# DeltaNet's triangular inverse: the 16x16 diagonal blocks are inverted on VectorE over 32 partitions, reached through DRAM, and TensorE does the levels 16, 32 and 64

## What is computed

```
qkv = silu(causal_depthwise_conv(proj[..., :DN_CONV_DIM], conv_w))
...
decay = exp(where(tri, g[..., :, None] - g[..., None, :], -inf))
k_beta = k * beta[..., None]
lower = where(strict, einsum("bhncd,bhnkd->bhnck", k_beta, k) * decay, 0.0)
a_mat = lower + eye(CHUNK)
sol = triangular_solve(a_mat, rhs, left_side=True, lower=True, unit_diagonal=True)
...
def step(state, xs):            # scan over the chunks
    v_new = u_n - w_n @ state
    o = q_n @ state + a_n @ v_new
    state = state * exp(gl_n) + k_n.T @ v_new
```

## Time and profile before

| | us |
|---|---|
| median of the 3 runs (lowest to highest) | 1511.27 (1500.47 to 1516.33) |
| the profiled execution's own time | 1499.67 |
| its span (first to last instruction) | 1497.7 |
| outside the span | 1.97 |
| DeltaNet's steps, of the span | about 51 to 454 |

### The profile page before, as it was taken

How to read it: one execution, slowest core, us unless ns; L and a number is a source line. 1 busy time by engine, 2 the same in 40 slices (tenths; PEclk the granted TensorE clock), 3 DMA queues, 4 the chain that set the end, 5 groups by cost and what they waited for, 6 DMA issues and landing times.

```text
span 1497.7 us, 19380 instructions
## 1 busy us (share of the span) xinstructions
PE 1455.9 (97%) x7270; PEld 1202.1 (80%) x7270; DVE 801.1 (53%) x1132; ACT 541.9 (36%) x820; POOL 268.0 (18%) x269
## 2 busy tenths in 40 slices
PE   7899999999989999999999999999999999999998
PEld 5788888888877888888888777866888888888877
DVE  5555666666647434334356587556443443434655
ACT  7334343434225314232243442244341322314344
POOL 5644444535203100000002120000200000000211
PEclk9999999999999999999999999769999999999998
DMA  6212121110112232323222328511323223232221
GB/s 174 60 29 57 29 57 40 44 49 21 43 56 92 92 112 85 112 84 103 94 85 86 111 57 169 113 29 43 113 85 112 85 92 105 84 112 85 85 85 56
DMA packets 163810, 120.73 MB, mean 81 GB/s; under 512 B 44417, under 2 KB 161442, under 8 KB 163746
## 3 DMA queue, kind: packets, MB, share of 16 engines
q1 hardware_dynamic: 152210, 116.71, 26.1%
q10 hardware_dynamic: 11536, 3.15, 1.0%
HBM read 112.50 MB, written 2.10 MB: 77 GB/s over the span
## 4 chain that ended last, share of the span: by engine, by line
PE 79%; DVE 10%; ACT 4%; issue 3%; DVEq 1%; DMA 1%; ACTq 1%; SPq 1%; POOL 0%; POOLq 0%
PE psum L148 22%; PE psum L150 22%; PE psum L149 21%; PE psum L830 3%; PE psum L821 3%; DVE wL L140 2%; ACT wH L132 1%; PE psum L837 1%; DVE bL L1274 1%; ACT taps L676 1%; DVE hT L1475 1%; PE psum L1828 1%; DVE acc L1473 1%; PE psum L784 1%; PE psum L785 0%
## 5 line engine op out<-in xcount | busy, mean ns | idle before, releaser
L148 PE MATMUL psum<-aH,wH 128*128 128x512 f32 x896 | 363.0, 405 | 5.2 <-DVE wL L140 3.2
L150 PE MATMUL psum<-aL,wH 128*128 128x512 f32 x896 | 350.6, 391 | 0.0
L149 PE MATMUL psum<-aH,wL 128*128 128x512 f32 x896 | 349.9, 391 | 0.0
L140 DVE TENSOR_TENSOR wL<-wRaw,wH 128x2048 fp32r<-128x2048 f32 (+2 forms) x126 | 250.7, 1993 | 135.5 <-ACT wH L132 129.9
L148 PE MATMUL psum<-bH,wH 128*128 128x512 f32 x720 | 285.0, 396 | 5.7 <-DVE pleT L1909 3.2
L150 PE MATMUL psum<-bL,wH 128*128 128x512 f32 x720 | 280.8, 390 | 0.0
L149 PE MATMUL psum<-bH,wL 128*128 128x512 f32 x720 | 280.6, 390 | 0.0
L132 ACT CAST wH<-wRaw 128x2048 fp32r<-128x2048 f32 (+2 forms) x110 | 199.2, 1815 | 192.0 <-PE psum L150 191.8
L148 PEld LDWEIGHTS psum<-aH,wH 128*128 128x128 f32 x896 | 169.2, 189 | 37.1 <-DVE wL L140 3.4
L150 PEld LDWEIGHTS psum<-aL,wH 128*128 128x128 f32 x896 | 168.6, 188 | 36.3
L149 PEld LDWEIGHTS psum<-aH,wL 128*128 128x128 f32 x896 | 169.2, 189 | 30.6 <-issue 0.5
(11 more groups left out here) (291 smaller groups left out, 1730.8 us busy)
## 6 DMA issues: line engine op xcount, KB each, us to landing
wRaw<-in_mlp_w_up SPq DMA_DIRECT2D x64, 512.0 KB
wRaw<-in_mlp_w_down SPq DMA_DIRECT2D x64, 512.0 KB
wRaw<-in_dn_w_in SPq DMA_DIRECT2D x32, 512.0 KB
wRaw<-in_ple_w_gate SPq DMA_DIRECT2D x16, 512.0 KB
wRaw<-in_sw_w_in SPq DMA_DIRECT2D x16, 256.0 KB
wRaw<-in_sw_w_out SPq DMA_DIRECT2D x16, 256.0 KB
wRaw<-in_dn_w_out SPq DMA_DIRECT2D x8, 384.0 KB
work<-in_x SPq DMA_DIRECT2D x4, 512.0 KB, 4.9
```

The costliest lines, as they stand in the source:

```text
L140: last = [nc.vector.tensor_tensor(o, r, h_.bitcast(F32), ALU.subtract) for o, r, h_ in zip(*([v if half is None else v[:, half * v.shape[1 ...
L148: nc.tensor.matmul(o, wh, xh, start=first, stop=False)
L149: nc.tensor.matmul(o, wl, xh, start=False, stop=False)
L150: return nc.tensor.matmul(o, wh, xl, start=False, stop=last)
```

## The change

The base of the inverse is now 16x16 blocks instead of 2x2, and LEVELS has three entries instead of six. Before level 16, the 32 diagonal blocks of a head (8 in each of 4 tiles) are inverted by DVE, one block on each of 32 partitions:

1. DVE writes the negated `lowT` (its subtraction in `grown` becomes an addition). SP sends it to DRAM (256 KB), waits, and reads the diagonal 16x16 blocks back, one to a partition (512 pieces of 64 bytes).
2. DVE inverts them by doubling within a partition: `pairs_inverse`, then `blocks_inverse(2)`, `(4)` and `(8)`, each two products (multiply with broadcast operands, then a sum over the inner axis), and `blocks_out` writes the transposed copy.
3. SP writes both forms to DRAM (2 x 512 pieces of 64 bytes, into two matrices whose other places were zeroed at the start), waits, and reads both whole as `inv` and `invT` (2 x 256 KB). `lower(0)` on PE waits for them (`blk_in`).

`base_tr` and ACT's first `inverse` are gone, with `x1_ok`. The orders are written anew: PE runs 23 units ahead of `lower(0)`, and `lower(0)` comes after `update(3)`; DVE has the block inverse between `advance(1)` and `advance(2)`; ACT's `taps_act(p, 0)` comes before `q_part(2)`; POOL's `taps_pool(p, 1)` before `os_pool`. The weight loads share SP's order with the new DMAs: `load_panel(a+2, 1)` and `load_panel(a+3, 0)` stand behind the blocks of head a. The diff, cut:

```diff
-        maskPair = sbd("maskPair", [P, P])
-        LEVELS = [2, 4, 8, 16, 32, 64]
+        LEVELS = [16, 32, 64]
...
+        B16 = LEVELS[0]
+        NB = NT * P // B16
+        BROW = B16 * (P + 1)
+        lowBlk = sbd("lowBlk", [P, B16 * (B16 + 1)])
+        blk = sbd("blk", [P, 2, B16 * (B16 + 1)])
+        terms = sbd("terms", [P, NB * BROW // P])
+        half = sbd("half", [P, (B16 // 2) ** 2])
+        lowD = nc.dram_tensor("low_blocks", [NB, BROW], F32, kind="Internal")
+        invD = nc.dram_tensor("inv_blocks", [2, NB, BROW], F32, kind="Internal")
...
-            v = maskPair[:].rearrange("p (a b) -> p a b", b=2)
-            keep(v, 0, [[-2, CH], [0, 2]], 1)
-            keep(v, 0, [[2, CH], [0, 2]], -1)
-            keep(v, -1, [[0, CH], [1, 2]], 0)
+            g.memset(terms[:], 0.0)
+            g.memset(blk[:], 0.0)
+            pool.drain()
+            g.memset(blk[:, 1, 0:B16 * B16:B16 + 1], 1.0)
+            pool.drain()
+            pool.sem_inc(blank_ok, 1)
...
+        def load_panel(sp, h, j):
+            sp.wait_ge(panel_lo, 2 * h + j - 1)
+            load_dn(sp, h, j)
+        def whole(d):
+            return d.rearrange("w (t b) r -> w t (b r)", t=NT)[:, :, 0:P * P].rearrange("w t (p c) -> p w t c", c=P)
+        def diagonal(d):
+            return d[:, :, 0:B16 * P].rearrange("w b (r c) -> b w r c", c=P)[:, :, :, 0:B16]
+        def blocks_sp(sp, a):
+            lo = lowD.ap().unsqueeze(0)
+            sp.wait_ge(low_ok, a + 1)
+            sp.dma_start(whole(lo)[:, 0], lowT).then_inc(low_out, 16)
+            sp.wait_ge(low_out, 16 * a + 16)
+            sp.dma_start(lowBlk[0:NB, 0:B16 * B16].rearrange("b (r c) -> b r c", c=B16), diagonal(lo)[:, 0]).then_inc(low_in, 16)
+            sp.wait_ge(blk_ok, a + 1)
+            for w in range(2):
+                sp.dma_start(diagonal(invD.ap())[:, w], blk[0:NB, w, 0:B16 * B16].rearrange("b (r c) -> b r c", c=B16)).then_inc(blk_out, 16)
+            sp.wait_ge(blk_out, 32 * a + 32)
+            for w, dst in enumerate((inv, invT)):
+                sp.dma_start(dst, whole(invD.ap())[:, w]).then_inc(blk_in, 16)
         def dn_sp(sp):
-            with sp.Fori(1, HEADS_A) as h:
-                for j in range(2):
-                    sp.wait_ge(panel_lo, 2 * h + j - 1)
-                    load_dn(sp, h, j)
-        def dn_out_sp(sp):
-            for m in range(4):
-                n = N_DNOUT + m
-                sp.wait_ge(panel_lo, n - 1)
-                dst = wRaw[:, n % 2, 0:EARLY * 256].rearrange("p (k n) -> p k n", k=EARLY)
-                v = dn_w_out[0][0:EARLY * P, 256 * m:256 * m + 256].rearrange("(k p) n -> p k n", p=P)
-                for q in range(2):
-                    ks = slice(q * EARLY // 2, (q + 1) * EARLY // 2)
-                    sp.dma_start(dst[:, ks, :], v[:, ks, :]).then_inc(panel_in[n % 2], PANEL_INC // 2)
+            sp.wait_ge(blank_ok, 1)
+            for w in range(2):
+                sp.dma_start(invD.ap()[w].rearrange("b r -> (b r)").rearrange("(p c) -> p c", p=P), terms[:]).then_inc(blank_out, 16)
+            for n in range(2, 5):
+                load_panel(sp, n // 2, n % 2)
+            sp.wait_ge(blank_out, 32)
+            with sp.Fori(0, HEADS_A - 3) as a:
+                blocks_sp(sp, a)
+                load_panel(sp, a + 2, 1)
+                load_panel(sp, a + 3, 0)
+            blocks_sp(sp, HEADS_A - 3)
+            load_panel(sp, HEADS_A - 1, 1)
+            dn_out_load(sp, 0)
+            blocks_sp(sp, HEADS_A - 2)
+            dn_out_load(sp, 1)
+            dn_out_load(sp, 2)
+            blocks_sp(sp, HEADS_A - 1)
+            dn_out_load(sp, 3)
+            dn_last_load(sp)
...
-        VTR = 2
+        VTR = 1
...
-            def base_tr():
-                pe.wait_ge(x1_ok, a + 1)
-                per_tile(lambda t: nc.tensor.transpose(bank[BZ][:, rng(t)], invT[:, t, :], ident[:])).then_inc(xtr_done, 1)
             def lower(i):
                 if i == 0:
-                    pe.wait_ge(xtr_ok, (NL + 1) * a + 1)
+                    pe.wait_ge(blk_in, 32 * a + 32)
                     pe.wait_ge(kd_ok, a + 1)
                 else:
                     pe.wait_ge(x_ok, NL * a + i)
...
-            fill(2)
+            fill(3)
             keys_tr()
             update(1)
+            fill(3)
+            walk(2)
+            fill(3)
+            solve(2)
+            fill(3)
+            update(2)
+            fill(3)
+            walk(3)
             fill(2)
-            walk(2)
+            solve(3)
             fill(2)
-            solve(2)
-            fill(2)
-            base_tr()
-            update(2)
-            fill(2)
-            walk(3)
-            lower(0)
-            solve(3)
-            fill(1)
-            corner(0)
             update(3)
-            fill(1)
-            for i in range(1, NL):
+            for i in range(NL):
                 lower(i)
-                inv_tr(i - 1)
+                if i:
+                    inv_tr(i - 1)
                 fill(1)
                 corner(i)
                 if i == VTR:
                     values_tr()
                 fill(2)
-                if i == NL - 2:
+                if i == VTR:
                     out_tr()
             inv_tr(NL - 1)
...
+            if p is not None:
+                taps_act(act, p, 0)
             q_part(2)
+            if p is not None:
+                tanh_act(act, p, 0)
+                taps_act(act, p, 1)
+            else:
+                prep_hi(act, n + 1, 0)
+            q_part(3)
+            tail(0)
+            if p is not None:
+                tanh_act(act, p, 1)
             inverse(0)
             if p is not None:
-                taps_act(act, p, 0)
-            q_part(3)
-            for i in range(1, NL):
-                inverse(i)
-                if i == 1:
-                    tail(0)
-                    if p is not None:
-                        tanh_act(act, p, 0)
-                        taps_act(act, p, 1)
-                if i == 2:
-                    prep_hi(act, n + 1, 0)
-                if i == 4 and p is not None:
-                    tanh_act(act, p, 1)
-            if p is not None:
                 taps_act(act, p, 2)
-            inverse(NL)
+                prep_hi(act, n + 1, 0)
+            inverse(1)
             tail(1)
+            inverse(2)
...
-                tt(inv, inv, t4(bank[BX]), ALU.subtract).then_inc(x_ok, 1)
+                tt(inv, inv, t4(bank[BX]), ALU.add).then_inc(x_ok, 1)
...
+            lb, xt, xm = lowBlk[0:NB], blk[0:NB, 1], blk[0:NB, 0]
+            def corners(buf, m):
+                q = buf.rearrange("p (q r) -> p q r", r=2 * m * (B16 + 1))[:, :, 0:2 * m * B16].rearrange("p q (k c) -> p q k c", c=B16)
+                return q[:, :, 0:m, 0:m], q[:, :, 0:m, m:2 * m], q[:, :, m:2 * m, m:2 * m]
+            def pairs_inverse():
+                dve.wait_ge(low_in, 16 * a + 16)
+                v.tensor_copy(xt[:, 1:B16 * B16:2 * B16 + 2], lb[:, 1:B16 * B16:2 * B16 + 2])
+                dve.drain()
+            def blocks_inverse(m):
+                nq = B16 // (2 * m)
+                tm = terms[0:NB, 0:nq * m ** 3].rearrange("p (q k i c) -> p q k i c", q=nq, k=m, i=m)
+                hf = half[0:NB, 0:nq * m * m].rearrange("p (q k i) -> p q k i", q=nq, k=m)
+                low = corners(lb, m)[1].rearrange("p q c i -> p q i c")
+                first, corner, second = corners(xt, m)
+                for left, right, out_ in ((low, first, hf), (second.rearrange("p q c i -> p q i c"), hf, corner)):
+                    if m == 2:
+                        for i in range(m):
+                            tt(tm[:, :, :, i], left[:, :, i].unsqueeze(2).to_broadcast([NB, nq, m, m]), right, ALU.mult)
+                    else:
+                        for q in range(nq):
+                            tt(tm[:, q], left[:, q].unsqueeze(1).to_broadcast([NB, m, m, m]),
+                               right[:, q].unsqueeze(2).to_broadcast([NB, m, m, m]), ALU.mult)
+                    dve.drain()
+                    v.tensor_reduce(out_, tm, AX, ALU.add)
+                    dve.drain()
+            def blocks_out():
+                r = xt[:, 0:B16 * B16].rearrange("p (k i) -> p i k", k=B16)
+                v.tensor_copy(xm[:, 0:B16 * B16].rearrange("p (i k) -> p i k", k=B16), r).then_inc(blk_ok, 1)
...
-            prep_lo(dve, n, 1, 0)
             dve.wait_ge(decC_ok, a + 1)
             dve.wait_ge(kk_done, a + 1)
-            tt(lowT, t4(bank[BZ]), decC, ALU.mult)
+            stt(out=work[:, 6, :], in0=bank[BZ], scalar=-1.0, in1=work[:, 7, :], op0=ALU.mult, op1=ALU.mult).then_inc(low_ok, 1)
+            prep_lo(dve, n, 1, 0)
             residual(1)
-            dve.drain()
-            tt(invT, lowT, bm(maskPair[:]), ALU.mult)
+            if p is not None:
+                g_next_dve(dve, p)
             solved(1)
-            dve.drain()
```

(81 more changed lines are left out.)

22 lines of the change are left out of this document (18 added, 4 removed).

## The result

| | before | after |
|---|---|---|
| median (lowest to highest) of 4 runs each, us | 1506.92 (1500.47 to 1516.33) | 1482.88 (1480.72 to 1483.17) |
| span of the profiled execution, us | 1497.7 | 1479.1 |
| ratio after to before, 95% interval | | 0.9853 (0.9808 to 0.9897) |

The change makes the kernel 1.5% faster. That is inside the range, 1467 to 1531, but well beyond my forecast of 0.998 (1504), and outside the 1493 to 1520 that I gave my likeliest case: it lies nearer to the rival with the shorter trip (1474).

A forecast was written before the change was run, and what follows sets the result against it. PE was taken to bound the DeltaNet step. Steady steps of 48.0 us against 47.8 (+1 over six) and head 7's gain of 4.4 summed to -3 us on 1499.67; forecast 1504 us (0.998), range 1467 to 1531.

The forecast's parts named there:

- my likeliest case: Trip back of about 7.8 us ahead of lower(0), clock lost; 1504 us, by itself 1493 to 1520; chance 0.40.
- the rival with the shorter trip: Writes 2.6, reads 2.7 us; lower(0) at 25.0, no clock loss, step 43.7; 1474 us; chance 0.27.
- the signs that I had set down for being wrong: Block writes landing in under 3 or over 6 us, blocks_out far from 20 us after solve(0), PE's clock holding.
- What bounds the kernel, what PE loses: PE sets the DeltaNet step; dropping three levels and base_tr takes 8.2 us off its 47.8, waits included.
- The first trip is hidden: lowT to DRAM and blocks back by 8.2 us after solve(0), before DVE arrives at 9.8; costs nothing.
- The block inverse and POOL: DVE's blocks_out ends at 17.9 undisturbed, 20.0 with waits for POOL: 1.7 in blocks_inverse(4), 0.4 in blocks_inverse(8).
- walk(3): PE stalls 1.3 us there, as advance(2) stands behind blocks_out in DVE's order.
- The way back: From blocks_out to lower(0): writes 4.0, reads 3.6, with handovers 7.8 us (bounds 4.9 and 12.6); stall 3.8.
- Short writes to DRAM are slow: Rival: the pair of block writes takes 8.8 us, the step 52.8; 1543 us; chance 0.25.
- After lower(0): masked(2) ends at 12.9 us after lower(0), corner(2) due at 11.4: PE stalls 1.5 us each step.
- The clock: The 3.8 us stall ahead of lower(0) halves PE's clock behind it, costing 1.6 us in each step.
- Head 7: No projection, so POOL is empty and PE's stall under 3 us; 4.4 us gained.

The follow-up runs named there:

- experiment 3: Kernel after, with POOL's three additions of the query taps replaced by one of 4 columns; last solve(0) at 408.2 us instead of 417.6.
- experiment 4: Kernel after, with 7 idle matmuls added on PE between update(3) and lower(0) to hold the clock; span 1484.5 us against 1479.1.
- experiment 7: Kernel after, with both halves of prep_lo(n+1, 0) behind grown(2) instead of one ahead of masked(2); last solve(0) at 408.5 us instead of 417.6.
- the last kernel but one: Kernel after, with taps_act(p, 0) behind q_part(2), lower(0) waiting for inv alone, prep_lo behind grown(2); median 1457.43 us, 0.970 of the kernel before.
- experiment 2: Kernel after, with the pair of block writes to DRAM done twice, one behind the other; span 1503.8 us against 1479.1.
- experiment 1: Kernel after, without the two block writes and with the two reads issued right behind the first trip; span 1472.7 us against 1479.1.
- the last experiment: The last kernel but one, with kDec moved behind advance(2); median 1460.40 us, 0.970 of the kernel before.

## Why the prediction was right in its course and short in its size

That the time fell inside the range is in part the range's width. Of the four cases I gave my own 0.40, and its time was missed by 21 us; what came is a case between it and the shorter trip (0.27). By two of the signs that I had set down for being wrong I was: the pair of writes landed in under 3 us, and PE's clock held in three of six steady steps. The third, blocks_out far from 20, did not come.

- **What bounds the kernel, what PE loses:** right. PE's busy time fell from 47.53 us in a period of 47.83 (the row below, of the kernel before) to 40.2 at full clock, 7.3 less; 8.2 with some 0.7 of waits was forecast.

```profile
150.85:198.68 47.83, 47.53 (x308) 40.66 (x308) 29.68 (x55) 19.43 (x32) 21.73 (x18) 1.00 0.17 45
```

- **The first trip is hidden:** right. 256 KB out and the blocks back took from 149.63 to about 154.2 (152.32 and the median 1.9 of this read), 7.5 us after solve(0) against 8.2, and DVE came at 9.5 against 9.8.
- **The block inverse and POOL:** blocks_out ended at 20.5 against 20.0. The 1.7 us for the second half of blocks_inverse(4) is 1.85 (2.26 less 0.41). The 0.4 for blocks_inverse(8) was put down to POOL; it is the products' own length (experiment 3), 0.34 in each of the two. The sum was right, one cause was not. The Trainium skill's rule (SBUF — State Buffer, "Who interferes with whom") that a reduction never waits for GpSimd, which no row before the change could show, agrees: in experiment 4 the products waited and the reduction beside POOL's additions took 0.28 us, against 0.27 with POOL idle.
- **walk(3):** a stall of 1.45 against 1.3, and 0.47 at update(2).
- **The way back:** the step that failed, by the slope. I had drawn 0.3 us for 128 pieces more from qS and kS and got 4.0 us for the pair of writes. It took 2.30, at the lower bound that I had passed over (2.2, if pieces cost nothing). I had called the two like transfers, but qS carries 64 KB and kS 32, neither goes to DRAM, and in the kernel after both land in 2.2 us: the 0.3 is not even steady from one trace to the next. The read of 512 pieces that I had put at 2.8 by the same slope took 1.9, as long as kS with 128 pieces and the same 32 KB. Against the 1.7 us saved stand blocks_out, 0.5 late, and the pair of reads, 3.7 to 4.3 against 3.6. lower(0) started at 26.5 to 27.15 instead of 27.8: 1.1 us in each steady step.
- **Short writes to DRAM are slow,** the rival of the other sign, with the rule on pieces under 512 bytes in the Trainium skill's DMA: Bandwidth & Descriptors, "Specifications": no such price shows here. (The doubling that I had worked with was my own assumption; the Trainium skill gives no factor there.) 32 KB in 512 pieces of 64 bytes landed 1.8 us after their issue, less than a store of 256 KB (2.4).
- **After lower(0):** 146.69 - 128.04 = 18.65 us to the next solve(0), at full clock, against 18.6. The masked(2) that comes late cost 1.07 where 1.5 was charged, and experiment 7 gave it back.
- **The clock:** the second step that failed. I had read from the earlier trace rows that a stall of 1.79 us keeps the clock and one of 2.94 loses it, and charged 1.6 us in each step for a stall of 3.8. The stalls were 1.7 to 2.4 us, and the clock fell in every second step, by 1.3 us. That is the other 0.95 us of a steady step. The price was near, the rule by length was not: a stall of 1.80 us lost the clock and one of 1.86 kept it in the kernel after, one of 2.38 kept it in experiment 7, and one of 3.09 in head 0 of the last kernel but one. With the stalls of 4.0 to 4.5 us of experiment 2 it was under 1.00 in all six steps. 1.1 + 0.95 over six steps are 12.3 of the 12.5 us by which the steady steps beat the forecast.
- **Head 7:** 7.1 us gained against 4.4. lower(0) started at 24.85 instead of 26.4, and from there to the next solve(0) it took 15.7 us, not the 17.1 of my sum, which had the decay and norms (2.6 us) of a next head that head 7 does not have, and lacked one unit that it does have.

The chain of the forecast stood in every stall, and experiments 1 and 2 show that the trip back is on it. Two terms of it were too long, the pair of writes and the clock, and both erred the same way; head 7 added 2.7 us to that and head 0, which I had taken at no change, 1.7.

## What to carry to other kernels

Where work is moved off the engine that binds, look for the chain that its result has to pass, and sum that chain with every operation of every queue that stands in it; the gain is what is left between the two. Here 8 us of PE a head became 1.9, and three small edits of order and waiting gave 3.5 more without touching the method. Do not price a transfer by a slope between two others that differ in bytes and in where they go; if one term decides, forecast from both of its bounds. Give each of two transfers its own semaphore, and put nothing between a product and its consumer that could as well run behind it.

## What the runs showed of the hardware

- A store to DRAM in 512 pieces of 64 bytes, from 32 partitions, lands 1.8 us after its issue, and two of them behind one another take 2.30 us. Reading such pieces took 1.9.
- VectorE's products with both operands in SBUF wait for a whole GpSimd operation each: two of 64 elements took 0.41 us alone, 2.26 and 2.52 beside the additions (1.28 us each).
- With stalls of 1.7 to 2.4 us in each step the clock fell in every second one; the same idle time kept it (1.86) and lost it (1.80). Idle time alone does not tell which. PE's two lines in the kernel after, each with the table by stage for its step:

```profile
220.30 1.16 PE L876 MATMUL psum<-xScaled,work 128*128 128x128 f32 x8 [1.86 <-DMA xScaled<-inv_blocks]
...
357.12 1.16 PE L876 MATMUL psum<-xScaled,work 128*128 128x128 f32 x8 [1.80 <-DMA xScaled<-inv_blocks]
```

```profile
193.60:238.82 45.22, 40.18 (x244) 33.83 (x244) 30.69 (x64) 17.48 (x28) 22.31 (x17) 1.00 0.26 66
...
330.51:377.00 46.49, 41.61 (x244) 35.15 (x244) 30.81 (x64) 17.47 (x28) 22.29 (x17) 0.96 0.18 53
```

- The attention stage runs with a granted clock that differs between executions of nearly the same program, and its length with it. Table by stage from its first matmul of kS and qS to the start of its last one that reads pleT, the same work each time, for the kernel before, the kernel after, experiment 1, and the last experiment:

```profile
956.98:1030.40 73.42, 68.20 (x319) 49.31 (x320) 43.50 (x138) 34.87 (x162) 0.00 (x0) 0.70 0.17 36
```

```profile
935.82:1011.59 75.77, 71.08 (x319) 51.37 (x320) 43.41 (x138) 34.87 (x162) 0.00 (x0) 0.66 0.16 35
```

```profile
915.51:1006.37 90.86, 88.61 (x319) 63.05 (x320) 43.47 (x138) 34.65 (x162) 0.00 (x0) 0.50 0.13 29
```

```profile
909.90:1000.07 90.17, 87.93 (x318) 62.71 (x319) 43.36 (x138) 34.58 (x162) 0.00 (x0) 0.51 0.14 29
```

  All the other kernels took 73.4 to 75.8 us here in their profiled executions. The two long ones are worth 15 us of span, almost the whole gain of this change, and no edit touches that stage. It is the likely source of much of the scatter between runs of one kernel, which was not tested.
